# Attention with the value product turned round, pairs of heads behind the scores, and coefficients spread across features

## The reference

```python
def masked_softmax(logits, mask, sink=None):
    z = jnp.where(mask, logits, -jnp.inf)
    m = jnp.max(z, -1, keepdims=True)
    if sink is not None:
        m = jnp.maximum(m, sink)
    e = jnp.where(mask, jnp.exp(z - m), 0.0)
    denom = jnp.sum(e, -1, keepdims=True)
    if sink is not None:
        denom = denom + jnp.exp(sink - m)
    return e / jnp.maximum(denom, 1e-30)
...
    o_a = banded_gqa(qa, ka, heads(v_a, A_KV), SWA_WINDOW, rel_bias[:, :A_HEADS], sinks)
    o_cmp, o_sel = nsa_cmp_sel(qb, k_cmp, v_cmp, k_sel, heads(vs, B_KV), bias_b)
    o_win = banded_gqa(qb, k_win, heads(vw, B_KV), NSA_WINDOW, bias_b, None)
    gb = jax.nn.sigmoid((g_b + b_nsa_gate).astype(jnp.float32)).reshape(Bn, S, B_HEADS, N_NSA_BRANCHES, 1)
    o_b = gb[..., 0, :] * o_cmp + gb[..., 1, :] * o_sel + gb[..., 2, :] * o_win
    y = jnp.concatenate([o_a.reshape(Bn, S, D_A) * jax.nn.silu(z_a.astype(jnp.float32)),
                         o_b.reshape(Bn, S, D_B) * jax.nn.silu(z_b.astype(jnp.float32))], axis=-1)
    out = y.astype(x.dtype) @ w_out
    return x + gate[:, None, :] * out
```

## Time and profile before

| | |
|---|---|
| median of 3 runs | 1449.93 us (1449.9 to 1450.42) |
| the profiled execution | 1452.35 us, span 1450.6 us |
| PE busy | 1424.3 us, 98% |
| PE weight loads | 1187.8 us, 82% |
| DVE busy | 742.1 us, 51% |
| ACT busy | 603.1 us, 42% |
| POOL busy | 113.1 us, 8% |
| attention, first score to last piece of the first output unit | 195.4 to 312.7 us |
| mean granted clock of PE | 0.995 |

### The profile page before, as it was taken

The page is one execution under the profiler, slowest core; times in us unless marked ns, Lnnn a source line. Parts: engine busy times, 40 slices in busy tenths (PEclk is TensorE's granted clock), DMA queues, the critical chain, the costliest instruction groups (busy, mean ns, idle before and its releaser), DMA issues.

```text
span 1450.6 us, 18082 instructions
## 1 busy us (share of the span) xinstructions
PE 1424.3 (98%) x6880; PEld 1187.8 (82%) x6880; DVE 742.1 (51%) x1200; ACT 603.1 (42%) x1014; POOL 113.1 (8%) x133
## 2 busy tenths in 40 slices
PE   6999999999999999999999999999999999999998
PEld 5787879998888888888888888888888888888887
DVE  6733678855666434556445344443457433333342
ACT  5624677745333332333333344432355333333221
POOL 5303232100000000000000111100000000000000
PEclk9999999999999999999999999999999999999999
DMA  9996200113433333212213233343332333333321
GB/s 283 318 228 216 65 1 2 59 59 104 159 101 93 109 89 101 87 59 76 77 52 87 71 89 88 101 150 98 87 102 83 106 102 101 88 98 96 105 80 58
DMA packets 227824, 149.69 MB, mean 103 GB/s; under 512 B 5330, under 2 KB 216014, under 8 KB 227108
## 3 DMA queue, kind: packets, MB, share of 16 engines
q1 hardware_dynamic: 223588, 131.63, 31.4%
q0 software_dynamic: 4160, 17.04, 4.1%
HBM read 140.92 MB, written 6.68 MB: 102 GB/s over the span
## 4 chain that ended last, share of the span: by engine, by line
PE 93%; DMA 2%; DVE 1%; SPq 1%; ACT 1%; issue 1%; DVEq 0%; ACTq 0%
PE ps L436 70%; PE ps L2266 6%; PE ps L2292 3%; PE ps L2191 3%; PE ps L1857 3%; DMA w_raw<-in_w_in_dram 2%; PE ps L2278 2%; PE ps L1965 1%; PE ps L1926 1%; PE ps L2177 1%; PE ps L2176 1%; SPq L550 1%; PE ps L1998 0%; SPq L580 0%; PE ps L2146 0%
## 5 line engine op out<-in xcount | busy, mean ns | idle before, releaser
L456 DVE TENSOR_TENSOR w_lo<-w_raw,w_hi 128x1024 fp32r<-128x1024 f32 (+1 forms) x214 | 258.3, 1210 | 255.8 <-ACT w_hi L451 253.1
L451 ACT ACTIVATE w_hi<-w_raw 128x1024 fp32r<-128x1024 f32 (+1 forms) x214 | 219.5, 1034 | 14.7 <-PE ps L436 11.2
L502 ACT ACTIVATE temps<-ps 128x512 f32<-128x512 f32 x67 | 40.0, 597 | 238.8 <-PE ps L436 238.8
L436 PE MATMUL ps<-g_hi,w_hi 128*128 128x512 f32 x384 | 95.8, 392 | 0.0
L436 PE MATMUL ps<-g_hi,w_lo 128*128 128x512 f32 x384 | 94.9, 389 | 0.0
L436 PE MATMUL ps<-g_lo,w_hi 128*128 128x512 f32 x384 | 94.8, 389 | 0.0
L436 PEld LDWEIGHTS ps<-g_hi,w_lo 128*128 128x128 f32 x384 | 72.1, 188 | 15.0
L436 PEld LDWEIGHTS ps<-g_lo,w_hi 128*128 128x128 f32 x384 | 72.1, 188 | 15.0
L436 PEld LDWEIGHTS ps<-g_hi,w_hi 128*128 128x128 f32 x384 | 71.5, 188 | 14.6
L436 PE MATMUL ps<-f_hi,w_lo 128*128 128x512 f32 x288 | 71.1, 389 | 0.0
L436 PE MATMUL ps<-f_hi,w_hi 128*128 128x512 f32 x288 | 71.1, 389 | 0.0
(11 more groups left out here) (448 smaller groups left out, 2738.7 us busy)
## 6 DMA issues: line engine op xcount, KB each, us to landing
w_raw<-in_w_in_dram SPq DMA_DIRECT2D x107, 512.0 KB, 3.9
w_raw<-in_w_ff_gate_dram SPq DMA_DIRECT2D x22, 512.0 KB, 3.7
w_raw<-in_w_ff_up_dram SPq DMA_DIRECT2D x22, 512.0 KB, 3.8
w_ada_shift_scale<-in_w_ada_dram SPq DMA_DIRECT2D x16, 512.0 KB, 8.3
w_raw<-in_w_r_out_dram SPq DMA_DIRECT2D x16, 512.0 KB, 4.5
w_raw<-in_w_ff_down_dram SPq DMA_DIRECT2D x16, 512.0 KB, 3.9
w_ada_gate<-in_w_ada_dram SPq DMA_DIRECT2D x4, 1024.0 KB, 11.6
x_spill<-x_t POOLq DMA_DIRECT2D x2, 2048.0 KB, 10.1
```

Source lines behind the costliest of these rows:

```text
L436: mm = pe.matmul(bank, w[:, slot, k], mov[:, at_k], start=first and n == 0 and k == 0, stop=last and n == 2 and k == kts - 1)
L451: act.activation(whi[:, slot, 0:kts], raw[:, slot, 0:kts], ACT.Copy).then_inc(hi_done, 1)
L456: nc.vector.tensor_tensor(wlo[:, slot, 0:kts], raw[:, slot, 0:kts], whi[:, slot, 0:kts].bitcast(F32), ALU.subtract).then_inc(lo_done, 1)
L502: act.activation(dst, ps[:, o % 4], func, scale=scale).then_inc(evac, 1)
```

## The change

Value product. V (128x64) becomes stationary and the turned probabilities (128 columns) move. The output is features by queries: two heads, neighbours of one key head, fill partitions 0 to 63 and 64 to 127 of a bank quarter. So the loop goes by 48 pairs. The heads of a group are reordered (n = 4g + j). A pair of up to two blocks shares one bank for its transposes and one copy (DVE in even pairs, ACT in odd ones), and its product stands three pairs behind its scores; a wider pair has two banks, two copies, and a distance of two. There are four score buffers and four of the turned probabilities, two of them in the raw weight slot of U_LAST; SP's load of output unit 3 therefore waits for the last product.

Coefficients. They now vary along the free axis. DVE makes them in pair 4G+5 (coefficients), POOL spreads them to 64 equal columns for a head (widen), PE turns them with four transposes after pair 8 and pairs 10, 14, ... 46 (coefficients_wide), ACT copies them out, DVE multiplies in the pair after (combined). The y tails need no transposes: POOL gates (y_gate), ACT rounds, POOL takes the rest.

Compressed branch. Its probabilities go to a tile of their own (csc); POOL multiplies them by gate and 1 over the sum ahead of the window keys' rests; PE turns them in pair 3; the product is turned as well (32 records of 128 columns, in pairs 6, 8, 10 and 12), and DVE only copies it.

The diff, cut to its core:

```diff
-CONVERT_AT = 61
-CO_PE_AT = ((0,), (2, 4), (10, 12), (16, 18))
+CONVERT_AT = 31
+CTR_AT = 3
+CO_PE_AT = (6, 8, 10, 12)
+K_WINDOW_AT = (2, 3, 4, 4)
+Y_AT = (15, 19, 22, 31, 34, 43, 46, 49)
+PAIRS = N_ATT // 2
+COEF_AT = (8,) + tuple(range(10, PAIRS, 4))
...
+def wide_pair(p):
+    return Step(2 * p).width > 2 * P
+def copies(p, engine):
+    return sum(wide_pair(n) or n % 2 == engine for n in range(p + 1))
+def pv_step(p):
+    return p + 2 if wide_pair(p) else p + 3
...
             for k in range(KT):
+                if k == 3:
+                    sp.wait_ge(m["pv_mm"], PAIRS)
                 load(None, 0, U_WO + k, w_out_v[:, :, k * P:(k + 1) * P])
...
+            pool.wait_ge(m["csoft_done"], 4)
+            pool.wait_ge(m["kl_done"], 5)
+            csc_heads = csc[:].rearrange("p g (q n) -> p (g q) n", n=NC_PAD)
+            g.tensor_tensor(csc_heads, csc_heads,
+                            cden[:].rearrange("p g q -> p (g q)").unsqueeze(2).to_broadcast([P, 32, NC_PAD]),
+                            ALU.mult).then_inc(m["cpool_done"], 1)
+            pool.wait_ge(m["cpool_done"], 2)
+            for part in range(4):
+                k_rest(2, part)
...
+            def widen(G):
+                pool.wait_ge(m["cf_done"], G + 1)
+                if G == 0:
+                    pool.wait_ge(unit_done, U_WO)
+                if G >= 2:
+                    pool.wait_ge(m["aux_tr"], G + 1)
+                g.tensor_copy(wide_of(G).rearrange("p t (h d) -> p t h d", h=2),
+                              coef[:, G % 2].rearrange("p (t h) -> p t h", h=2).unsqueeze(3).to_broadcast([P, 4, 2, HD])
+                              ).then_inc(m["cpool_done"], 1)
...
+                if 0 <= p < PAIRS and (wide_pair(p) or p % 2 == 0):
+                    dve.wait_ge(m["t_mm"], 2 * p + (1 if wide_pair(p) else 2))
+                    pt_free(dve, p)
+                    w = att(2 * p).width if wide_pair(p) else 2 * att(2 * p).width
+                    v.tensor_copy(pt_of(p)[:, 0:w], ps[:, 2, 0:w]).then_inc(m["pt_d"], 1)
...
+                if n >= 5 and (n - 5) % 4 == 0 and n < PAIRS:
+                    coefficients((n - 5) // 4)
+                if n == PAIRS:
+                    coefficients(N_GROUPS - 1)
+                if n - 1 in COEF_AT:
+                    combined(COEF_AT.index(n - 1))
...
+            def weighted(n):
...
+                for b in range(blocks):
+                    c = (u.first_block + b) * P + u.g * HD
+                    for half in range(2):
+                        mm = pe.matmul(ps[half * HD:half * HD + HD, 4 + u.group % 2, blk(n % 4)], proj[:, v, c:c + HD],
+                                       pt_of(n, half)[:, blk(b)] if wide_pair(n) else pt_of(n)[:, blk(half * blocks + b)],
+                                       start=b == 0, stop=b == blocks - 1)
+                mm.then_inc(m["pv_mm"], 1)
+            def coefficients_wide(G):
+                pe.wait_ge(m["cpool_done"], G + 3)
...
+                for t in range(4):
+                    mm = trans(ps[:, 6, blk(t)], wide_of(G)[:, t])
+                mm.then_inc(m["aux_tr"], 1)
+            for n in range(PAIRS + 1):
+                if n < PAIRS:
+                    scored(2 * n)
+                    scored(2 * n + 1)
+                if n == 0:
+                    v_local()
+                for p in (n - 3, n - 2):
+                    if p >= 0 and pv_step(p) == n:
+                        weighted(p)
+                if n >= 1:
+                    transposed(2 * n - 2)
+                    transposed(2 * n - 1)
+                if n == CTR_AT:
+                    compressed_transposed()
+                if n in CO_PE_AT:
+                    compressed_out(CO_PE_AT.index(n))
+                if n in COEF_AT:
+                    coefficients_wide(COEF_AT.index(n))
+            early_out(0)
+            weighted(PAIRS - 1)
+            coefficients_wide(N_GROUPS - 1)
```

More of the change, by code:

```diff
@@ L141, in att @@
     return Step(s)
-def tails_at(s):
-    return [(i, half) for i in range(NI) for half in range(2)
-            if s == (24 * i + 29 + 3 * half if i < NI - 1 else 24 * i + 13 + 17 * half)]
 class Own:
@@ new lines, in transposed @@
+            def transposed(t):
+                p, half = divmod(t, 2)
+                w = att(t).width
+                pe.wait_ge(m["s_exp"], t + 1)
+                before = p - 1 if wide_pair(p) or wide_pair(max(p - 1, 0)) else p - 2
+                if half == 0 and before >= 0:
+                    for engine, name in enumerate(("pt_d", "pt_a")):
+                        if copies(before, engine):
+                            pe.wait_ge(m[name], copies(before, engine))
+                for b in range(w // P):
+                    bank, c = (2 + half, b) if wide_pair(p) else (2 + p % 2, half * w // P + b)
+                    mm = trans(ps[:, bank, blk(c)], sc_of(t)[:, blk(b)])
+                mm.then_inc(m["t_mm"], 1)
```

483 lines of the change are left out of this document (256 added, 227 removed).

## The result

The changed kernel is slower: 1455.87 us median (1454.71 to 1458.51, 6 runs) against 1449.97 for the kernel before (1449.83 to 1450.75), a ratio of 1.0042 with a 95% interval of [1.0029, 1.0054]. The forecast was 1442.9 us with a range of 1435.0 to 1455.0. Direction and range were both wrong. The profiled execution of the changed kernel has a span of 1454.5 us, 10.9 above the 1443.6 of the forecast; the one before had 1450.6.

The account below looks back on a forecast made before the run. PE bounds the kernel, except in i = 0. For i = 1 to 3, 17.7 saved less 9.0 switches and 1.2 transposes gives 7.5; less 0.7 idle, plus 0.3 at i = 0, about 7: 1449.9 - 7 = 1442.9 us, range 1435.0 to 1455.0.

Parts of the forecast that it names:

- The turned product: Value product in the attention: 432 records fall from 0.104 to 0.058 us each, saving 19.9 us.
- The switches: PE changing between full-width and half-width work for 48 pairs: 0.25 us a pair, 12.0 us in all.
- Idle before, in i = 1 to 3: PE's idle time in the attention's groups with two to four blocks: some 6 us before, 6.7 after.
- i = 0: Tokens 0 to 127, one key block: POOL's chain sets the end, pair 12 starts at 215.1 us, gain 0.3.
- The clock: PE at 1.2 GHz for some 3 us from 215.5 us; a second such stretch costs about 1 us.
- The signs of being wrong: Records above 0.073 us, an edge above 0.2 us, or PE idle between 195 and 306 us far from 10 us.
- The tail: End of the attention: the last coefficient's chain outlasts early_out(1) by 0.9 to 1.4 us, leaving PE idle.
- Coefficients late in two-block groups: Five two-block groups: the spread coefficients come after PE wants them, some 0.8 us each, 4.0 in all.
- SP's late load: Loads of output units 3 to 5 held until the last product: costs nothing, unit 3 wanted over 10 us later.
- A: Each group outside i = 0 waits 0.7 us longer than counted on other engines: 1449.2 us; chance 0.18.
- B: Half-width records don't shorten: loss from 0.073 us on, 1453.5 us at 0.08, 1464 at 0.106; chance 0.13.
- C: One edge hides in waits (4.8 us) or narrow groups run at PE's pace (2.5): 1436 to 1438 us; chance 0.17.

Follow-up runs that it names:

- halves_in_turn: Changed kernel with the product's loops exchanged, all blocks of the first half and then all of the second: 1462.42 us in one execution.
- gates_on_scalar: Changed kernel with the addition of 1 to the gates moved from VectorE to ScalarE: 1453.02 us, 1.0020.
- late_first_gates: Changed kernel, coefficients turned a pair later (except last but one), conversions at pair 41, key roundings at pairs 0, 2, 3, 4, gates' addition on ScalarE: 1448.74 us, 0.9989.
- filler_at_start: Changed kernel with 17 extra transposes of the identity (the filler) in PE's idle time in pairs 0 and 1: 1454.71 us, 1.0027.
- coefficients_later: Changed kernel with PE's turning of the coefficients, and the copy, combining and rounding of y, one pair later: 1453.44 us, 1.0019.
- late_filled_spread: Changed kernel with coefficients_later (last but one kept at pair 46), conversion_later, filler, and key roundings at pairs 2, 3, 5, 6: 1452.76 us, 1.0013.
- conversion_later: Changed kernel with the two weight conversions moved from pairs 31 and 32 to 41 and 42: 1455.67 us, 1.0028.
- coefficient_step_out: late_first_gates with VectorE's multiplication of coefficients by gates left out for the selected and window branches, 8 times: 1445.10 us, 0.9961.
- coefficient_on_gpsimd: late_first_gates with the eight multiplications of coefficients by gates moved from VectorE to GpSimd, nothing left out: 1446.21 us, 0.9975.

## Why the prediction was wrong

**The turned product: right.** 0.055 us a record against 0.058, and halves_in_turn shows what it rests on, the alternation. By its pitch the product takes 432 x 0.055 = 23.8 us, against the 45 that I counted before. By busy time, in which every record counts to its end, it is 61.8 us before and 17.5 + 17.1 = 34.6 after (rows of before, then after: busy us, mean ns):

```profile
L2191 PE MATMUL ps<-proj,probs_t 128*128 128x64 f32 x432 | 61.8, 271 | 2.6 <-ACT probs_t L1038 2.3
...
L2340 PE MATMUL ps<-probs_t,proj 128*64 128x128 f32 x216 | 17.5, 288 | 1.6 <-ACT probs_t L1153 1.0 <-issue 0.7
L2340 PE MATMUL ps<-w_raw,proj 128*64 128x128 f32 x216 | 17.1, 284 | 0.9 <-ACT w_raw L1153 0.9
```

**The switches: right at four blocks, short at two.** Score to first product record, and last record to turning, have the 0.10 us gaps. A four-block pair takes 2.97 us and 3.48 before; the terms of the sum give 3.48 - 16 x 0.046 + 0.25 = 2.99, and the 2.9 that the prediction named was a slip. A two-block pair takes 1.65 us, where the terms give 1.70 - 8 x 0.046 + 0.25 = 1.58. In 20 such pairs that is 1.4 us. On the other side this part has 40 transposes for 32, not 36 for 24, which is 0.4 us less work than forecast. These two account for most of the 1.1 us by which PE's gain in i >= 1 fell short, 6.4 us instead of 7.5.

**Idle before, in i = 1 to 3: this step failed.** I wrote that PE's idle "is some 6 us in this part (a group at two blocks takes 7.6 to 8.1 us for 8 x 0.85 = 6.8)" and only 0.7 more afterwards. The difference of 0.8 to 1.3 us a group was mostly work that 8 x 0.85 leaves out: coefficient and y transposes, output pieces, half-clock time. The busy column in the same says it: 8.10 of 8.10, 7.20 of 7.60. The idle before was 1.1 us. The idle after was forecast at 6.7 and is 7.3. So 4.9 us were lost in a subtraction and 0.6 in the idle after; with PE's 1.1 us and the moved product's 1.0 that is the whole miss of 7.6 us in this part. That the sum for the idle after came so near is partly luck: the waits for POOL were 2.6 us where 4.0 were forecast and the tail 0.9 where 1.4 were, and waits for ScalarE's copies away from the weight conversions, 1.6 us, were not forecast at all. With 1.1 in its place, the same working gives a gain of 7.5 - 5.6 + 0.3 = 2.2 us, 1447.7.

**i = 0: this step failed too.** Group 3 was to start at 215.1 and started at 218.39. Its pairs take 1.13 us of PE, as forecast; POOL's chain, on which I spent the argument, was not what came last. What came last was VectorE's addition of 1 to the gates, held by POOL's running key rest. The kernel before has this instruction too. There it began at 196.07, between POOL's third rest (1.29 us from 194.72, so to 196.01) and the fourth, and took 0.20; the first score now comes 2.75 us behind the start of POOL's rests and not 3.57, 0.8 us nearer as forecast, so that the addition came at 195.70, with POOL's last rest running until 196.77. gates_on_scalar puts the price at 3.1 us in groups 0 and 1, clock included. With it i = 0 lasts 21.3 us. In late_first_gates, where ScalarE's key roundings are also spread, it lasts 20.3 us, and the forecast had 20.5.

**The sum of the misses.** 7.6 us in i = 1 to 3 and 3.3 in i = 0 are the 10.9 us between the two spans. The other 2.1 us of the 13.0 between forecast and median have no cause in the profile: the profiled execution of the changed kernel has a span 1.4 us under the median, where the forecast took 0.7 above.

**The clock: mechanism right, size wrong.** "A second such stretch costs about 1 us, in the range, not a case." It stood at half for some 6.9 us, and filler_at_start puts it at about 2 us. It was a case: of the changed kernel's six executions the three with a mean clock of 0.996 took 1454.7 to 1455.5 us, the three with 0.992 to 0.994 took 1456.3 to 1458.5. Where in these the clock fell wasn't recorded, so that this widens the spread to 3.8 us is likely, not shown.

**The signs of being wrong.** None of the three clearly came: records at 0.055 us, edges at 0.10, and 7.8 us of idle between 195 and 306 us. All three looked at the kernel after. The term that failed was the idle before, and no sign was set on it.

**The tail: right.** 0.9 us of idle ahead of the last tokens, forecast 0.9 to 1.4.

**Coefficients late in two-block groups: place right.** PE did wait for POOL's widening, 2.6 us in three places, where 0.8 us in each of five groups was forecast. That one pair more of distance removes it (coefficients_later) should have been seen from my own sentence that VectorE makes them just as PE wants them. The late weight conversions cost 2.4 us in group 8, of which I gave 1.3: the second conversion took 2.32 us beside POOL, not 1.22.

**SP's late load: right.** Nothing behind the output unit changed.

**The rivals.** A (the other engines take it all) had the right mechanism and the wrong end: its price per group was put on top of an idle time that was itself wrong by 5 us, so it stopped at 1449.2. It should have ended on the slower side. B was refuted by the 0.055 us between records. C didn't come: both edges stayed at 0.10 us, and the narrow groups took longer than before; its second branch, 2.5 us, would by itself give 1440.4 us and not 1436 to 1438.

**What held steps.** VectorE's additions, subtractions and multiplications with all operands in SBUF were stretched when a step of POOL was running: 0.20 to 1.13 us, 0.17 to 1.29, 1.22 to 2.32. Reciprocals, and copies that read PSUM, were not (0.75 at 194.74 in gates_on_scalar, and 0.68 at 210.98 in the changed kernel, both beside POOL). The two small steps end within 0.1 us of POOL's. The subtraction of the weight conversion ends 1.08 us behind POOL's step, about its own length, in the changed kernel:

```profile
264.93 2.32 DVE L506 TENSOR_TENSOR w_lo<-w_raw,w_hi 128x1024 fp32r<-128x1024 f32 x1
...
264.90 1.27 POOL L840 TENSOR_TENSOR y_f<-out_a,proj 128x512 f32<-128x512 f32 x1
```

The Trainium skill (SBUF — State Buffer, "SBUF: two separate sides") says that VectorE and GpSimd share one pair of ports as an exclusive lock that is held for a whole instruction, and that a GpSimd step blocks a VectorE step in a two-port mode, or one with two SBUF inputs if the GpSimd step reads SBUF too. The three rows agree in that none of the steps ends before POOL's does. The addition of 1 has a single input, so by that rule only the two-port mode is left for it; no row here shows an instruction's mode.

## What to carry to other kernels

An estimate of idle time must be read from the busy column and not from length less the work one has thought of, and a sign of being wrong must be set on the figures of the kernel before too. When a change gives GpSimd more to do beside VectorE, look at every small SBUF-to-SBUF step of VectorE that stands ahead of something urgent, whatever its own length: here one step of 0.2 us cost 3.1 us at the wrong place, clock included, and eight others 2.8 us together. Moving the one to ScalarE and the eight to GpSimd's own queue, with coefficients turned a pair later, key roundings spread and weight conversions moved to the four-block groups, turned 1.0042 into 0.9975, and 0.9965 with the filler. A change that is sound for the bound engine still needs its order worked out anew for the others.

## What the runs showed of the hardware

- Half-width matmuls (fp32, 64 columns stationary) with 128 moving columns: 0.055 us each if the two halves of the array alternate, 0.087 us if one half's come in a row.
- A VectorE multiplication of 128x8 elements with both inputs in SBUF, 0.17 us alone, takes up to 1.29 us beside a GpSimd step; a reciprocal of 128x96 beside one stays at 0.75.
- The granted clock fell to half behind idles of 0.62 and 1.16 us and stayed there for about 6.9 us. Where these gaps were filled with turnings of the identity it did not fall there, though it did later behind an idle of 2.95 us (late_filled_spread). Behind the tail's idle of 0.9 us it fell in some profiled executions (conversion_later, coefficient_step_out) and not in others (the changed kernel, coefficient_on_gpsimd); behind one of 1.12 us in gates_on_scalar it did not.
